# A decoder step: the final states of the retention branch, made at the end of the program instead of in its middle

## The reference, cut to what matters

```
kd = k * exp((t_len - 1 - t) * log_gamma)      # each key decayed to the end of the prompt
s  = exp(t_len * log_gamma) * s0 + kd^T v      # 64 x 64 per head; s0 is zero for the prompt
```

## Time and profile before

| | us |
|---|---|
| median of three runs | 790.13 |
| the profiled execution, its own time | 791.83 |
| its span (first to last instruction) | 789.8 |
| PE (TensorE) busy | 767.3 |
| DVE (VectorE) busy | 384.2 |
| POOL (GpSimd) busy | 295.9 |
| ACT (ScalarE) busy | 225.1 |
| granted TensorE clock, mean over the span | 0.987 of full speed |

### The profile page before, as it was taken

The page is one execution under the profiler, slowest core; times in us unless marked ns, Lnnn a source line. Parts: engine busy times, 40 slices in busy tenths (PEclk is TensorE's granted clock), DMA queues, the critical chain, the costliest instruction groups (busy, mean ns, idle before and its releaser), DMA issues.

```text
span 789.8 us, 14330 instructions
## 1 busy us (share of the span) xinstructions
PE 767.3 (97%) x5281; PEld 549.4 (70%) x5281; DVE 384.2 (49%) x719; ACT 225.1 (29%) x436; POOL 295.9 (37%) x221
## 2 busy tenths in 40 slices
PE   9999999999999999999999999999999899999992
PEld 7887778676677888777777787888887744333330
DVE  4637777677397789544544112734533722031210
ACT  4131344342423355132414223422201511020100
POOL 0000331364563984354425554534241112332314
PEclk9999999999999899999999999999999999999997
DMA  9242762345566442245534453352682699999933
GB/s 364 116 161 82 210 193 82 89 155 167 169 187 199 150 151 66 61 156 183 176 124 132 152 179 130 102 191 69 227 332 100 234 340 412 368 391 370 384 110 50
DMA packets 72538, 148.32 MB, mean 188 GB/s; under 512 B 13335, under 2 KB 47144, under 8 KB 70420
## 3 DMA queue, kind: packets, MB, share of 16 engines
q1 hardware_dynamic: 65716, 135.43, 49.7%
q0 software_dynamic: 5920, 10.82, 5.4%
q10 hardware_dynamic: 832, 1.16, 0.6%
HBM read 137.71 MB, written 18.90 MB: 198 GB/s over the span
## 4 chain that ended last, share of the span: by engine, by line
PE 92%; DVE 4%; ACT 1%; DMA 1%; issue 1%; POOLq 0%; POOL 0%; SPq 0%; DVEq 0%; ACTq 0%
PE ps L893 22%; PE ps L627 17%; PE ps L1253 11%; PE ps L862 7%; PE ps L1139 6%; PE ps L1325 5%; PE ps L670 3%; PE ps L642 3%; PE ps L919 2%; PE ps L616 2%; PE ps L1242 2%; PE ps L697 1%; PE ps L726 1%; PE ps L713 1%; DMA tmp<-in_xT 1%; PE ps L969 1%
## 5 line engine op out<-in xcount | busy, mean ns | idle before, releaser
L627 PE MATMUL ps<-xn,ring 128*128 128x268 f32 (+1 forms) x576 | 136.5, 391 | 0.2 <-ACT qk L1419 0.2
L627 PEld LDWEIGHTS ps<-xn,ring 128*128 128x128 f32 x576 | 107.0, 190 | 24.4 <-issue 4.2
L2632 POOL TENSOR_TENSOR kv<-kv,sgd 128x1024 f32<-128x1024 f32 (+1 forms) x32 | 81.5, 2561 | 97.8 <-DVE tmp L1892 52.5
L1571 ACT ACTIVATE sgt<-sgt,vec 128x260 f32<-128x260 f32 x60 | 30.1, 510 | 122.9 <-DVE sgt L2173 70.8
L2747 POOL DMA_INDIRECT out_y<-cst,gtab x24 | 37.3, 1555 | 70.4 <-DVE cst L2544 41.2
L862 PE MATMUL ps<-br,ring 128*128 128x260 f32 x256 | 62.9, 395 | 0.7 <-DVE sgt L2177 0.7
L893 PE MATMUL ps<-xn,ring 128*128 128x260 f32 x240 | 58.0, 385 | 0.0
L893 PE MATMUL ps<-xn,qb 128*128 128x260 f32 x240 | 57.6, 383 | 0.1
L862 PEld LDWEIGHTS ps<-br,ring 128*128 128x128 f32 x256 | 48.9, 194 | 11.7 <-issue 3.2
L1920 DVE TENSOR_REDUCE sgd<-kv 128x32 f32<-128x1024 f32 (+1 forms) x32 | 40.6, 1278 | 21.5 <-POOL kv L2632 21.5
L893 PEld LDWEIGHTS ps<-xn,qb 128*128 128x128 f32 x240 | 45.4, 190 | 7.4 <-issue 0.4
(11 more groups left out here) (534 smaller groups left out, 1507.6 us busy)
## 6 DMA issues: line engine op xcount, KB each, us to landing
ring<-in_w_mg SPq DMA_DIRECT2D x32, 640.0 KB, 4.4
kv<-in_kc SPq DMA_DIRECT2D x128, 128.0 KB, 2.1
kv<-in_vc SPq DMA_DIRECT2D x128, 128.0 KB, 2.1
ring<-in_w_in SPq DMA_DIRECT2D x24, 512.0 KB, 4.7
kv<-in_w SPq DMA_DIRECT2D x8, 1024.0 KB, 12.6
br<-in_w SPq DMA_DIRECT2D x7, 1024.0 KB, 13.9
sgd<-in_w SPq DMA_DIRECT2D x6, 1024.0 KB, 13.1
qk<-in_w SPq DMA_DIRECT2D x6, 1024.0 KB, 9.5
```

What stands on the lines that cost most here:

```text
L627: mm = pe.matmul(ps[:, 2 * (t % 2) + h, 0:hw], wsl(c, k), xnv[:, k, col0 + h * hw:col0 + (h + 1) * hw], start=(k == 0), stop=(k == KT - 1))
L1571: act.activation(g, g, ACT.Sigmoid, bias=vv(V_BM + 8 * "ABCD".index(n) + m + i)).then_inc(g_a, 1)
L2632: pool.tensor_tensor(kb, kb, qbc[:, b:b + 1, :].to_broadcast([P, HALF // 2 + (half and u), 256]), ALU.mult)\
```

## The change

The decayed keys and the values are written to two scratch tensors in memory, and read back during the last quad of experts into buffers that are free by then; the states are made from them behind the last expert output. ScalarE issues the four writes behind the event `kd_ok`, ahead of the evacuation of `GC0`. SyncE issues the four reads behind the last expert weights. The states go to bank 2; ScalarE copies them out and also issues their store. What waited for the states to be copied, because `tmp` and `vtok` are overwritten (VectorE ahead of clearing `vtok`, ScalarE ahead of the squares into `tmp`), now waits for the four writes (`kd_out`). GpSimd's wait and store between units 27 and 28 are gone.

```diff
+        scr_k, scr_bv = scratch("scr_k", (P, NB, 256)), scratch("scr_bv", (P, NB, 256))
...
+        kd_late, bv_late = view(sgd, 2048, NB, 256), view(br, 2048, NB, 256)
...
-        kv0, rst_out, rs_out = sem("kv0"), sem("rst_out"), sem("rs_out")
+        kv0, kd_dma, rs_out = sem("kv0"), sem("kd_dma"), sem("rs_out")
+        kd_out, kd_in = (kd_dma, 64), (kd_dma, 128)
...
             for n in range(STREAM, 12 * QUADS):
                 weights_used(n - STREAM)
                 weights(n)
+            weights_used(12 * QUADS - STREAM + 2)
+            sp.wait_ge(*kd_out)
+            sp.dma_start(kd_late[:, 0:4, :], scr_k[:, 0:4, :]).then_inc(kd_dma, 16)
+            sp.dma_start(kd_late[0:TAIL, 4, :], scr_k[0:TAIL, 4, :]).then_inc(kd_dma, 16)
+            sp.dma_start(bv_late[:, 0:4, :], scr_bv[:, 0:4, :]).then_inc(kd_dma, 16)
+            sp.dma_start(bv_late[0:TAIL, 4, :], scr_bv[0:TAIL, 4, :]).then_inc(kd_dma, 16)
...
-            for stored, n in ((kv_out, 3), (rst_out, 1), (rs_out, 1), (outs, POOL_OUTS)):
+            for stored, n in ((kv_out, 3), (rs_out, 1), (kd_dma, 9), (outs, POOL_OUTS)):
...
-            def ret_states(heads):
-
-                pe.wait_ge(*kd_ok)
-                pe.wait_ge(ob_ev, 2)
-                for h in heads:
+            def ret_states():
+
+                pe.wait_ge(*kd_in)
+                for h in range(H):
                     for b in range(NB):
                         rows = P if b < 4 else TAIL
-                        mm = pe.matmul(ps[0:64, 7, h * 64:h * 64 + 64], kdv[0:rows, b, h * 64:h * 64 + 64],
-                                       vt[0:rows, b, 256 + h * 64:256 + h * 64 + 64], start=(b == 0), stop=(b == NB - 1))
-                if H - 1 in heads:
-                    mm.then_inc(st_mm[0], 1)
+                        mm = pe.matmul(ps[0:64, 2, h * 64:h * 64 + 64], kd_late[0:rows, b, h * 64:h * 64 + 64],
+                                       bv_late[0:rows, b, h * 64:h * 64 + 64], start=(b == 0), stop=(b == NB - 1))
+                mm.then_inc(st_mm[0], 1)
...
             def ret_samples():
 
                 pe.wait_ge(*rs_ok)
+                pe.wait_ge(ob_ev, 2)
...
-                if (name, end) == ("GC0", 0):
-                    ret_states(range(2))
...
             for m in range(2):
-                gate_tile("C", m, beside)
+                gate_tile("C", m)
                 if m == 0:
                     ret_samples()
-                    ret_states(range(2, H))
                     pe.wait_ge(br_ok, 1)
...
                 outputs(q, 1)
                 outputs(q, 2)
+            ret_states()
...
                 act.wait_ge(gla_t, GT["so"])
-                act.wait_ge(rst_out, 16)
...
+                act.wait_ge(*kd_out)
                 for t in range(2):
                     act.activation(bn[:, t, :], brv[:, 2 + t, :], ACT.Square).then_inc(b_sq, 1)
...
+            act.wait_ge(*kd_ok)
+            act.dma_start(scr_k[:, 0:4, :], kdv[:, 0:4, :]).then_inc(kd_dma, 16)
+            act.dma_start(scr_k[0:TAIL, 4, :], kdv[0:TAIL, 4, :]).then_inc(kd_dma, 16)
+            act.dma_start(scr_bv[:, 0:4, :], vt[:, 0:4, 256:512]).then_inc(kd_dma, 16)
+            act.dma_start(scr_bv[0:TAIL, 4, :], vt[0:TAIL, 4, 256:512]).then_inc(kd_dma, 16)
             for m in range(2):
                 copy(f"GC{m}", sgtv[:, m, :], HN, ACT.Sigmoid, bias=vv(V_BM + 16 + m))
...
-                    act.wait_ge(*st_mm)
-                    act.activation(rst, ps[0:64, 7, 0:256].rearrange("p (h v) -> p h v", h=H), ACT.Copy).then_inc(st_ev[0], 1)
...
+            act.wait_ge(*st_mm)
+            act.activation(rst, ps[0:64, 2, 0:256].rearrange("p (h v) -> p h v", h=H), ACT.Copy).then_inc(st_ev[0], 1)
+            act.wait_ge(*st_ev)
+            act.dma_start(o["ret_p"], rst).then_inc(kd_dma, 16)
...
-            dve.wait_ge(*st_ev)
+            dve.wait_ge(*kd_out)
             dve.wait_ge(s_v, 16)
             dve.wait_ge(kv_out, 48)
             dve.memset(vtok[:, 0:2048], 0.0)
...
-                if x == K_LAST + 2:
-                    pool.wait_ge(*st_ev)
-                    pool.dma_start(o["ret_p"], rst).then_inc(rst_out, 16)
```

More of the change, by code:

```diff
@@ L1359, in _ @@
                 pe.wait_ge(m_yd, TILES)
+                pe.wait_ge(*st_ev)
                 with pe.Fori(0, n_over) as i:
```

## The result

The changed kernel takes 793.14 us (median of 20 runs, 790.1 to 794.74), the kernel before on the same chip 789.71 (20 runs). The ratio is 1.0039, with a 95% interval of 1.0027 to 1.0051: slower by 0.4%, about 3.1 us. I had forecast 785.0, in a range of 783.3 to 787.5.

A forecast was written before the change was run, and what follows sets the result against it. TensorE (PE) bounds the kernel, busy 767.3 of 789.8 us. Instructions 4.14 plus clock 2.5 minus a stand of 1.5 gave 5.1 us, so the median 790.13 becomes 785.0; range 783.3 to 787.5.

The forecast's parts named there:

- Nothing behind it is bound to a fixed time: Behind VectorE's L2184 and TensorE's X3: every load waits for TensorE's or VectorE's progress, so the 5 us gain is kept.
- So 5.1 us reaches the expert stage: From the middle to the expert stage: TensorE arrives there 5.1 us earlier, the whole predicted gain.
- 4.14 us removed, 1.5 in the stand before LA, clock 1.00 through 262.: Around GC0: forty instructions leave TensorE's chain, TensorE waits about 1.5 us for VectorE's mean subtractions, clock stays high.
- the clock falls all the same: Rival, chance 0.13: the clock falls at 254 us again despite the states being gone; among the two said to gain three.
- GpSimd gains 0.9 only: GpSimd's last unit, held by pages and row L442, ends at 266.1 instead of 266.96; `s2` leaves X6 0.8 margin.
- deadlines of units 28 and 29: Their key pages are due at 254.7 and 257.0 us; a delay of at most 3.9 us from the writes fits.
- VectorE is tight, a tie at X5 and X3.: VectorE's `t1` and X5 both at 274.3; at L2184 VectorE 281.9 against X3 281.5; nothing counted as lost.
- my second rival: Rival, chance 0.15: VectorE's work collides with GpSimd's; among the two said to gain three.
- 2.5 us back from the clock.: Gate and branch tiles at 254 to 262 us: at full clock L862 takes 1.85 instead of 3.77, L616 1.85 instead of 2.44.
- slower, by the writes: Rival, chance 0.05: `kd_out` holds VectorE ahead of L2047; gain gone if the last write lands beyond 263.2, 793 at 266.
- Tail hidden, reads free, writes 0 (0 to 1).: States at the end finish between 779 and 783, before the span's end at 784.7; reads and middle writes cost 0 us.

The follow-up runs named there:

- kernels without transfers: Changed kernel with the states left out (no writes, reads, matmuls, copy), without and with 80 instructions put back before LA's wait: 1.0024 and 0.9981 of the kernel before.
- masks' experiments: GpSimd's mixer D masks moved behind 297 us: changed kernel plus 80 instructions 0.9974, also with value writes at 138 us 0.9970; kernel before, masks alone 0.9999.
- experiment with 20 matmuls: Changed kernel with 20 one-column matmuls (80 instructions) put before TensorE's wait for LA's banks: 789.72 us, 1.0000 of the kernel before.
- shifted kernel: Kernel before, with 6 of 12 warm-up matmuls replaced by 50 one-column ones, moving TensorE's stream by 176 instructions: 797.18 us, 1.0093 of the kernel before.

## Why the prediction was wrong

The step that failed is *"Nothing behind it is bound to a fixed time [...] So 5.1 us reaches the expert stage"*. GpSimd's list bound the second X6, and the shifted instruction stream cost a stand and a fall of the clock behind L1003, together 3.1 us. By its steps, measured against the profile that it used:

- *4.14 us removed, 1.5 in the stand before LA, clock 1.00 through 262.* Right in both profiles of the changed kernel: the stand was 1.32 and 1.01, and the second gate tile began 5.2 us earlier (I had 5.1). That the clock stays up was luck in part, as it fell there in three other kernels without the states in the middle; so my rival "the clock falls all the same" can come true in single executions. The gain of three that my range gives it was an estimate that no run shows; the three falls that came there cost 1.7 us each (3.4 us at 0.50).
- *"GpSimd gains 0.9 only", margin 0.8 at X6.* Wrong by 1.4. I had bounded the writes' effect on the key pages by the deadlines of units 28 and 29, and taken the time of the row L442 as fixed. SyncE's last eight pages were issued from 256.59 instead of 254.82 and the row at 262.80 instead of 261.06; the last unit ended at 267.4, not 266.1. TensorE lost 0.7 us at the first X6, which began at 271.38 and not at 270.7. Of the 1.8 us by which the pages were late, 0.4 to 1.0 were there in the kernels without transfers too; what delayed them there is open.
- *"Nothing behind it is bound to a fixed time."* This is the sentence that cost most of the gain. I followed VectorE to X3 and left out GpSimd's list behind the first sum. Before, GpSimd waited 2.46 us for TensorE ahead of its sum L2683 at 277.77 and had no other idle time of note until the second `s2`, which ended at 290.73, 1.5 us ahead of the X6 that reads it at 292.22. Five microseconds could not pass through that:

```profile
277.77 1.28 POOL L2683 TENSOR_TENSOR qb<-ring,qb 128x512 f32<-128x512 f32 x1 [2.46 <-PE ps L893]
```

Against the second profile of before, `s2` ends at the same time (288.89 and 288.99), and TensorE keeps just the 1.5 by which the X6 stood behind it:

```profile
274.02 1.92 PE L893 MATMUL ps<-cx,qb 128*128 128x260 f32 x8
287.72 1.27 POOL L2676 TENSOR_TENSOR qb<-qb,ring 128x512 f32<-128x512 f32 x1
290.47 1.92 PE L893 MATMUL ps<-cx,qb 128*128 128x260 f32 x8
```

The traces of the masks' experiments show this cause.

- *VectorE is tight, a tie at X5 and X3.* It held nobody. The long L2056 (3.28 us), on which this and my second rival rested, was that of one execution: it took 1.24 in the two other profiles of before, and 1.26 and 1.24 in those of the changed kernel. GpSimd's L2693 overlaps it in all three profiles of before (2.01 us, from 271.98, 271.56 and 271.22). No run shows that GpSimd's work lengthens it; that, and the gain of three that my range gives the rival, were my estimate.
- *2.5 us back from the clock.* Its size was that of one execution. In the two further profiles of before LA begins 1.8 us earlier, so 0.7 of the 2.5 is left, and where the clock doesn't fall nothing is. The profiled execution (791.83) took 3.0 and 3.6 us longer than the two did. I had subtracted the gain of that execution from a median of others.
- *"So 5.1 us reaches the expert stage."* 3.4 us reached 397.5 us (1.7 against the second profile). There the shift of the stream cost 1.66 us of stand and 1.7 of clock. The experiment with 20 matmuls measures both at 3.1 us in the medians. This is as much as the distance between the changed kernel and the one before, and no term or rival of mine had it. My rival "slower, by the writes" had the right side with the wrong mechanism: `kd_out` held nobody.
- *Tail hidden, reads free, writes 0 (0 to 1).* The tail was right. The transfers together cost 1.2 to 1.5 us in the medians, which the intervals don't resolve, and put the second `s2` some 1.2 to 2.1 us later in the traces. That is above my bound, and by way of GpSimd and not of VectorE.

The sum that the runs support, the changed kernel's profile against the second one of before: TensorE is 3.4 us ahead at LA, 2.6 at the first X6, 1.5 at the second, 1.7 at L1003, and 1.6 us late when the clock is back at 405 us. Both executions have one fall of the clock up to there. The medians say 3.1 us late. The record points to falls of the clock for the other 1.5 us, by three numbers.

First, how much the change gains depends on the fall near 254 us in the kernel before. Measured from the start of GC0, its second X6 begins after 49.96 us with the long fall, 48.39 and 48.42 with the short one, and 46.83 in the shifted kernel, without a fall; the changed kernel's begins after 46.59 and 46.41. Beside an execution without the fall, the whole change is worth 0.2 to 0.4 us at that place:

```profile
294.16 1.92 PE L895 MATMUL ps<-cx,qb 128*128 128x260 f32 x8
```

Second, the granted clock of single executions is on record. Its mean is 0.9886 over the 20 of the changed kernel, and 0.9906, 0.9927 and 0.9907 over 29, 23 and 28 of the kernel before on the three later occasions (it is not on record for the 20 that ran beside the change). The difference of 0.0020 to 0.0041 is 1.6 to 3.2 us of a span of 790, one or two short falls of 1.7. The falls at 632 us, in one of the two profiles of the changed kernel and in one of the three of before, are some of them.

Third, the second profile of the changed kernel has one fall before the end, as has the second of before, and took 790.44 us against 788.80: 1.6 more, as at 405 us. So 1.6 + 1.6 = 3.2 us is my estimate of the distance; that the second term is falls of the clock is worked out and not tried by a run.

## What to carry to other kernels

Work taken out of a saturated engine must be followed through every engine that feeds it until each has idle time to give: here GpSimd had waited 2.5 us for TensorE, and could not deliver five earlier. Taking 80 instructions out of TensorE's 10,562 also moved the places at which its blocks are fetched (42 of 16 KB, one per 256 instructions by the count), and that cost 3.1 us here; behind an edit of a long unrolled program, look for bursts of tiny matmuls (4.8 ns an instruction in this one), and for a stand without a releaser there, and try a few idle instructions before judging the edit. And what one profiled execution shows of the clock is subtracted only from that execution, or taken from several: the long fall near 254 us was in one of three profiles of the kernel before.

## What the hardware showed

TensorE ran out of instructions in five executions of this case. The 128 matmuls of L1003 with their 128 weight loads are consumed in 1.24 us, 4.8 ns each, while a block of 256 took 2.4 to 2.7 us from the start of its transfer to its first instruction. So in this burst they are consumed faster than a block arrives, and the cost is up to 2.03 us of stand, with a fall of the clock behind the four longest stands (1.52 to 2.03 us) and none behind that of 0.38.

The falls of the clock to its lower level (0.50 in the windows) lasted 3.4 or 6.8 us wherever work followed: 254 to 258 and 254 to 261 in the same kernel, 401 to 405 in the changed one, 404 to 412 in the kernel before with the shift. Near 254 us the kernel before had a long fall in one profile and a short one in two, and with the shift it had none.
